# A decoder layer on one Trainium2 core: places of their own for three output-weight tiles, and query tiles that begin on half of the blocks

## What is computed

```python
proj = x @ w_in                                   # 1024 x 8208
y_a = rms_norm(gla(q_a, k_a, v_a, decay)) * silu(r_a)
y_b = attention(rope(q_b), rope(k_b), v_b)        # 8 heads, causal
y = sigmoid(gate_a) * y_a + sigmoid(gate_b) * y_b
x1 = layer_norm(ALPHA * x + y @ w_out, ln1_g, ln1_b)
qry = x1 @ w_q                                    # 8 heads x 2 x 128
s = einsum('nhpd,pkd->nhpk', qry, sub_keys)       # 2 x 128 scores for each head
# top 16 of each half, top 16 of their sums: expert ids and softmax gates
hid = gelu(x1 . u_tab[expert]);  h = sum(gate * hid * v_tab[expert])
out = layer_norm(ALPHA * x1 + h, ln2_g, ln2_b)
```

## Time and profile before

| | us |
|---|---|
| median of 3 runs (1089.97 to 1090.32) | 1090.04 |
| the profiled execution | 1089.23 |
| its span, first to last instruction | 1087.4 |
| PE busy | 1071.9 (99%) |
| DVE busy | 791.6 (73%) |
| ACT busy | 610.2 (56%) |
| POOL busy | 173.0 (16%) |

### The profile page before, as it was taken

The page is one execution under the profiler, slowest core; times in us unless marked ns, Lnnn a source line. Parts: engine busy times, 40 slices in busy tenths (PEclk is TensorE's granted clock), DMA queues, the critical chain, the costliest instruction groups (busy, mean ns, idle before and its releaser), DMA issues.

```text
span 1087.4 us, 18011 instructions
## 1 busy us (share of the span) xinstructions
PE 1071.9 (99%) x5604; PEld 905.8 (83%) x5604; DVE 791.6 (73%) x1516; ACT 610.2 (56%) x1114; POOL 173.0 (16%) x120
## 2 busy tenths in 40 slices
PE   9999999999999999999999999999999999999996
PEld 6887888687888888888888999988888888888885
DVE  4457767387999989899999988875555555555556
ACT  4337645465556756666676666665455555545553
POOL 3040002203000002233224445510000000000001
PEclk9999999999999999999999999999999999999999
DMA  8554444253455554444444434445666555555553
GB/s 281 186 193 161 134 152 145 97 174 136 155 172 187 187 189 159 171 155 160 168 155 139 151 135 142 148 155 194 203 203 207 198 193 193 193 193 193 193 193 116
DMA packets 52857, 186.48 MB, mean 171 GB/s; under 512 B 6336, under 2 KB 6976, under 8 KB 52816
## 3 DMA queue, kind: packets, MB, share of 16 engines
q1 hardware_dynamic: 51152, 181.82, 49.3%
q0 software_dynamic: 944, 3.15, 0.8%
q10 hardware_dynamic: 720, 1.05, 0.3%
HBM read 184.94 MB, written 1.05 MB: 171 GB/s over the span
## 4 chain that ended last, share of the span: by engine, by line
PE 72%; issue 12%; POOL 6%; DVE 5%; DMA 2%; ACT 2%; POOLq 0%; ACTq 0%; SPq 0%; DVEq 0%
PE ps L1514 13%; PE ps L1611 10%; PE ps L1610 10%; PE ps L1612 10%; PE ps L1516 7%; POOL hot_j L464 5%; PE ps L1266 5%; PE ps L1268 4%; PE ps L1267 4%; PE ps L1565 3%; DVE wlo L788 1%; PE ps L1327 1%; ACT whi L487 1%; DMA xraw<-xT 1%; DMA raw<-w_tiles_in 1%
## 5 line engine op out<-in xcount | busy, mean ns | idle before, releaser
L788 DVE TENSOR_TENSOR wlo<-raw,whi 128x1024 fp32r<-128x1024 f32 x341 | 427.0, 1253 | 247.6 <-ACT whi L487 245.2
L487 ACT ACTIVATE whi<-raw 128x1024 fp32r<-128x1024 f32 x343 | 363.2, 1060 | 292.3 <-DMA raw<-w_tiles_v 165.3
L1514 PE MATMUL ps<-pair,whi 128*128 128x512 f32 x1152 | 412.8, 401 | 0.1
L1516 PE MATMUL ps<-pair,wlo 128*128 128x256 f32 x1152 | 321.5, 279 | 0.0
L1514 PEld LDWEIGHTS ps<-pair,whi 128*128 128x128 f32 x1152 | 216.4, 188 | 47.7 <-issue 0.3
L1516 PEld LDWEIGHTS ps<-pair,wlo 128*128 128x128 f32 x1152 | 217.3, 189 | 0.0
L1610 PE MATMUL ps<-whi,hhi 128*128 128x512 f32 x512 | 199.3, 389 | 0.4 <-DVE wlo L788 0.4
L1612 PE MATMUL ps<-whi,hlo 128*128 128x512 f32 x512 | 199.2, 389 | 0.0
L1611 PE MATMUL ps<-wlo,hhi 128*128 128x512 f32 x512 | 199.2, 389 | 0.0
L464 POOL TENSOR_TENSOR hot_j<-raw_ij,gateT 128x512 f32<-128x512 bf16 x64 | 120.0, 1875 | 334.1 <-DVE raw_ij L1171 334.1
L671 ACT ACTIVATE low<-ps 128x256 f32<-128x256 f32 x144 | 55.1, 383 | 137.4 <-PE ps L1516 136.0
(11 more groups left out here) (212 smaller groups left out, 891.2 us busy)
## 6 DMA issues: line engine op xcount, KB each, us to landing
raw<-w_tiles_u SPq DMA_DIRECT2D x128, 512.0 KB, 3.2
raw<-w_tiles_v SPq DMA_DIRECT2D x128, 512.0 KB, 3.2
raw<-w_tiles_in SPq DMA_DIRECT2D x63, 512.0 KB, 3.3
raw<-w_tiles_q SPq DMA_DIRECT2D x16, 512.0 KB, 3.2
raw<-w_tiles_out SPq DMA_DIRECT2D x8, 512.0 KB, 3.2
xt<-x POOLq DMA_DIRECT2D x1, 1024.0 KB, 7.2
raw<-w_tiles_in SPq DMA_DIRECT2D x2, 256.0 KB, 4.4
xraw<-xT SPq DMA_DIRECT2D x2, 256.0 KB, 7.6
```

The costliest lines, as they stand in the source:

```text
L487: act.activation(whi[:, tile.slot, :], raw[:, tile.slot, :], ACT.Copy)\
L788: dve.tensor_tensor(wlo[:, tile.slot, :], raw[:, tile.slot, :], whi[:, tile.slot, :].bitcast(F32), ALU.subtract)\
L1514: pe.matmul(ps[:, bank, :], whi[:, tile.slot, cols], pair[:, k, :, :].rearrange("p a n -> p (a n)"), start=k == 0, stop=False)
L1516: last = pe.matmul(ps[:, bank, SEQ:2 * SEQ], wlo[:, tile.slot, cols], ahi[:, k, :], start=False, stop=k == KC - 1)
```

## The change

**Places of their own.** Out tiles 5, 6 and 7 no longer go through the ring. They get buffers in memory that the attention has finished with (`apart_raw`, `apart_hi`, `apart_lo`), semaphores of their own, and loads which SP issues between the last eight tiles of `w_in`. So T_Q falls from 72 to 69: q tile 0 waits for the slot of out tile 1, q tiles 1 and 2 for those of 2 and 3, q tile 3 for that of out tile 4, and q tile 4 for that of q tile 0.

**Tail.** The out tail is four tiles instead of three.

**Order of ACT, POOL and DVE.** ACT's copies of q tiles 0, 1 and 2 all stand ahead of the norm. POOL makes the low parts of all three ahead of its share of the norm. DVE no longer treats both column halves of token half 1 at each step but one after the other, with x1's low parts 0 and 1 between; the last norm takes the new order too.

**q tiles 0 to 2 on half of the blocks.** Once parts 0 and 1 are there, PE runs blocks 0 to 3 of q tile 0, in three groups of 256-column matmuls, then of q tiles 1 and 2, with the transposes of parts 2 and 3 between; then blocks 4 to 7 of the three.

```diff
+APART, Q_AHEAD = 3, 3
-T_Q = T_OUT + TILES_OUT
+T_Q = T_OUT + TILES_OUT - APART
-TAIL = 3
+TAIL, TAIL_OUT = 3, 4
...
+        loads(0, TILES_IN - 2 * NS, w_tiles_in, 1)
+        for m in range(TILES_IN - 2 * NS, TILES_IN):
+            load(Tile(m), w_tiles_in[m, :, :])
+            n, odd = divmod(m - (TILES_IN - 2 * NS), 2)
+            if odd and n < APART:
+                sp.wait_ge(S["gl_mm"], 1)
+                sp.dma_start(apart_raw[n][:, :], w_tiles_out[TILES_OUT - APART + n, :, :])\
+                    .then_inc(apart_full[n], 16)
...
-        split_lo_q(Tile(T_Q))
+        for n in range(Q_AHEAD):
+            split_lo_q(Tile(T_Q + n))
         pool.wait_ge(S["in_ln1"], 32)
         ln_apply(0, g1b, b1b, "ln_done0")
-        split_lo_q(Tile(T_Q + 1))
...
-        for k in range(TILES_OUT - AHEAD + 1):
-            split_hi(Tile(T_OUT + k + AHEAD))
+        for k in range(TILES_OUT - AHEAD + Q_AHEAD):
+            n = k + AHEAD - (TILES_OUT - APART)
+            if n < 0:
+                split_hi(Tile(T_OUT + k + AHEAD))
+            elif n < APART:
+                apart_high(n)
+            else:
+                split_hi(Tile(T_Q + n - APART))
...
-        norm(0, OUTB, LN1_BANKS, "x1_bank", "g1_ready", T_Q, "ln_done")
-        x1_low()
+        norm(0, OUTB, "x1_bank", ("out_done", 1))
+        dve.wait_ge(S["g1_ready"], 4)
+        weigh(0, LN1_BANKS)
+        root(0)
+        shifted(0, LN1_BANKS, "ln_done")
+        weigh(1, LN1_BANKS)
+        x1_low(0)
+        x1_low(1)
+        shifted(1, LN1_BANKS, "ln_done")
+        x1_low(2)
+        x1_low(3)
+        dve.sem_inc(S["lo_ready"], Q_AHEAD)
...
-        by_pairs(Tile(T_Q), HID[0], True)
+        turn_x1(0)
+        turn_x1(1)
+        blocks, slot = range(KC // 2), Tile(T_Q).slot
+        pe.wait_ge(S["act_split_hi"], X_PARTS + 4 + 2)
+        for k in blocks:
+            cols = slice(k * P, (k + 1) * P)
+            pe.matmul(ps[:, HID[0], 0:SEQ], whi[:, slot, cols], ahi[:, k, :], start=k == 0, stop=False)
+            pe.matmul(ps[:, HID[0], SEQ:2 * SEQ], wlo[:, slot, cols], ahi[:, k, :], start=False, stop=False)
+        turn_x1(2)
+        pe.wait_ge(S["act_split_lo"], X_PARTS + 4 + 2)
+        for k in blocks:
+            cols = slice(k * P, (k + 1) * P)
+            pe.matmul(ps[:, HID[0], SEQ:2 * SEQ], whi[:, slot, cols], alo[:, k, :], start=False, stop=False)
         pe.wait_ge(S["lo_first_q"], 2)
-        for k in range(4):
+        pairs(Tile(T_Q + 1), HID[1], blocks)
+        turn_x1(3)
+        pe.wait_ge(S["lo_first_q"], 3)
+        pairs(Tile(T_Q + 2), HID[2], blocks)
+        pe.wait_ge(S["act_split_lo"], X_PARTS + 4 + 4)
+        for k in range(Q_AHEAD):
+            pairs(Tile(T_Q + k), HID[k], range(KC // 2, KC)).then_inc(S["tiles_used"], 1)
+            if k > 0:
+                scores(k - 1)
+        for k in range(Q_AHEAD - 1, 4):
             by_pairs(Tile(T_Q + k + 1), HID[(k + 1) % 4])
             scores(k)
```

More of the change, by code:

```diff
@@ L330, in layer @@
     raw_full = [S[f"raw_full{n}"] for n in range(NS)]
+    apart_full = [S[f"apart_full{n}"] for n in range(APART)]
     in_xT = [S[f"in_xT{n}"] for n in range(X_PARTS)]
@@ L1001, in _, with norm @@
                 y_low(3)
-        def norm(n, banks, gain, bank_done, gain_ready, tiles, done):
+        def norm(n, banks, bank_done, last_done):
             def total(t, half):
@@ L1028, in norm, with weigh @@
             total(1, 0)
-            dve.wait_ge(S["tiles_used"], tiles)
+            dve.wait_ge(S[last_done[0]], last_done[1])
             total(1, 1)
             variance(1)
-            dve.wait_ge(S[gain_ready], 4)
-            halves = [slice(half * CW, (half + 1) * CW) for half in range(2)]
-            for half, cols in enumerate(halves):
-                own.step(dve.scalar_tensor_tensor(out=xt[:, 1, cols], in0=xt[:, 1, cols], scalar=mv[:, 1, 0:1],
-                                                  in1=ps[:, gain[0] + half, :], op0=ALU.subtract, op1=ALU.mult))
+        def weigh(half, banks):
+            xs = xt[:, 1, half * CW:(half + 1) * CW]
+            own.step(dve.scalar_tensor_tensor(out=xs, in0=xs, scalar=mv[:, 1, 0:1], in1=ps[:, banks[0] + half, :],
+                                              op0=ALU.subtract, op1=ALU.mult))
@@ L1037, in norm, with root @@
+        def root(n):
             dve.wait_ge(S["ln_sqrt"], NT * n + 2)
             own.do(dve.reciprocal(rstd[:, 1:2], rstd[:, 1:2]))
[L1039 to L1053 removed]
@@ L1055, in _, with shifted, x1_low @@
-        dve.wait_ge(S["in_x"], 16)
-        norm(0, OUTB, LN1_BANKS, "x1_bank", "g1_ready", T_Q, "ln_done")
-        x1_low()
+        def shifted(half, banks, done):
+            own.wait()
+            xs = xt[:, 1, half * CW:(half + 1) * CW]
+            dve.scalar_tensor_tensor(out=xs, in0=xs, scalar=rstd[:, 1:2], in1=ps[:, banks[1] + half, :],
+                                     op0=ALU.mult, op1=ALU.add).then_inc(S[done], 1)
+        def x1_low(n):
+            j, t = divmod(n, NT)
+            dve.wait_ge(S["act_split_hi"], X_PARTS + 4 + n + 1)
+            part = (slice(None), slice(4 * j, 4 * j + 4), slice(t * P, (t + 1) * P))
+            dve.tensor_tensor(alo[part], ps[:, OUTB[2 * t + j], :].rearrange("p (k n) -> p k n", n=P),
+                              ahi[part].bitcast(F32), ALU.subtract).then_inc(S["act_split_lo"], 1)
@@ L1254, in _ @@
             split_lo(Tile(m))
-        norm(1, VB, LN2_BANKS, "out_bank", "g2_ready", T_END, "out_ready")
+        norm(1, VB, "out_bank", ("tiles_used", T_END))
+        dve.wait_ge(S["g2_ready"], 4)
+        weigh(0, LN2_BANKS)
+        root(1)
+        shifted(0, LN2_BANKS, "out_ready")
+        weigh(1, LN2_BANKS)
+        shifted(1, LN2_BANKS, "out_ready")
     @block.tensor
@@ L1487, in _ @@
         for half in range(2):
-            for k in range(TILES_OUT - TAIL, TILES_OUT):
-                last = out_half(Tile(T_OUT + k), k, 1, (half,))
-                if half == 1:
+            for k in range(TILES_OUT - TAIL_OUT, TILES_OUT):
+                last = out_half(k, 1, (half,))
+                if half == 1 and k < TILES_OUT - APART:
                     last.then_inc(S["tiles_used"], 1)
+                if half == 1 and k == TILES_OUT - 1:
+                    last.then_inc(S["out_done"], 1)
             if half == 0:
```

101 lines of the change are left out of this document (56 added, 45 removed).

## The result

The changed kernel takes 1092.76 us (median of 8 runs, 1091.99 to 1095.17) against 1089.99 (8 runs beside them, 1088.53 to 1090.73): a ratio of 1.003, interval 1.0021 to 1.004. It is **slower, by 2.8 us**. The predicted time was 1091.8, 1.75 above the kernel before; the measured one lies in the predicted range, but beyond the border of 0.2%, where I had given "slower" only 0.28. In a second batch the same kernel took 1092.44, 1.0021 (1.0012 to 1.003), 2.2 us more than before.

A forecast was written before the change was run, and what follows sets the result against it. PE was taken to bound the kernel. Q tile 1's scores, held by q tile 4's later load, come 1.75 us late, the out stage's 0.1 included: median 1090.04 becomes 1091.8 us, range 1090.1 to 1093.0.

The forecast's parts named there:

- the border of 0.2%: Whole kernel: about 2.2 us, the least a measurement can tell from no change; slower begins at 1092.2 us.
- What bounds it, and the mark: PE, busy 1071.9 of 1087.4 us, bounds; delay of q tile 1's scores, at 268.37 us before, is the kernel's loss.
- Out stage, +0.1: Out tiles: wait at tile 7 goes, 0.68 us wait at tile 5 comes; stage ends 252.75 instead of 252.63.
- (d): Rival: apart loads or their waits hold a w_in or out tile; one landing of 3.3 us, 1095; chance 0.02.
- (c): Rival: POOL's first low part starts before DVE's third; PE waits 2.5 us at out tile 7; 1094.3; chance 0.03.
- 256-column matmuls: First halves of q tile 0: 0.115 us each; if each waited for a weight load, twelve cost 0.9 us more.
- the chain of 5.33 us from q tile 0 to the scores of q tile 1: q tile 4's load, ACT's copies, DVE's query: q tile 0 ends 2.25 us later, PE idles 2.2, mark +1.75.
- Rival (a): Scores of q tile 1 not held, load and copies being quicker; mark at 267.9, time 1089.5; chance 0.14.
- It stays hidden: Norm: POOL, stretched by DVE's subtraction, may be 0.5 us later in everything, yet its x1 parts come before PE wants them.
- It costs from the point at which the granted clock of the pause reads below 1.00: Rival: clock falls to 1.2 GHz in PE's pause before q tile 1's scores; +2.8 us more, 1094.6; chance 0.05.
- The sum: Whole kernel: +1.75 us, out stage's +0.1 included; median from 1090.04 to 1091.8.
- same: Whole kernel: time within what a measurement cannot tell from no change, up to 1092.2 us; chance 0.70.

The follow-up runs named there:

- low_first: Changed kernel with ACT copying the low products of q tiles 1 and 2 ahead of its copies of q tiles 4 and 5; 1091.15 us, 1.0009 of the kernel before.
- whole: Changed kernel, but PE makes all four transposes first and then does q tiles 0 to 2 whole; 1090.89 us, 1.0006 of the kernel before.
- one_input: Changed kernel with DVE's shift rewritten to one tensor operand and a per-partition scalar; 1091.80 us, 1.0021 of the kernel before.
- after: The changed kernel itself, first batch, against the kernel before; 1092.76 us, ratio 1.003.
- after_again: The changed kernel unaltered, run again in a second batch against the kernel before; 1092.44 us, ratio 1.0021.
- two_then: Changed kernel with POOL making the low part of q tile 2 behind its share of the norm; 1091.56 us, 1.0014 of the kernel before.
- warm_q: Changed kernel with nine unused matmuls filling PE's pause ahead of the scores of q tile 1; 1091.99 us, 1.0017 of the kernel before.

## Why the prediction was right and wrong

- **What bounds it, and the mark: right.** The delay of the scores of q tile 3 against the kernel before orders the kernels nearly as their times do (0.1 us: +0.2 and +0.3; 0.3 to 0.9: +0.7 to +0.9; 1.7 to 2.4: +1.7 to +2.3; 3.8 and 3.9: +2.2 and +2.8). No trace shows that time was given back later.
- **Out stage, +0.1: right.** PE waits 0.67 us (forecast 0.68) at the first apart tile instead of at out tile 7, and the stage takes 0.15 us more. No PE wait on the apart loads is to be seen; (d) and (c) did not happen.
- **256-column matmuls, and the chain of 5.33 us from q tile 0 to the scores of q tile 1: right.** They go 0.12 us apart, the chain takes 5.30 us, the pause is 2.05 us (forecast 2.2), and low_first removes it. Rival (a) is out.
- **"It stays hidden", said of POOL's work ahead of the norm: the step that failed first.** I followed POOL's queue and its ports against DVE's large subtraction and did not look at what small instructions of DVE fall into POOL's 7.6 us. `shift` did, with two tensor operands in SBUF: 1.76 us for 0.16. Through DVE's own order, in which the sums of token half 1 stand behind it, it delayed the first transposes of that half by 0.6 us and the mark by 0.4 to 0.6; only in whole, which has all four transposes first, did it also show through ACT and POOL. With it repaired (one_input) the mark is 17.38 for a computed 17.35.
- **"It costs from the point at which the granted clock of the pause reads below 1.00": the condition was right, its chance was not.** I took the end of the kernel as evidence that the clock outlives a pause of 2 us, and gave the fall 0.05. It fell in about one execution in four or somewhat more, and in both profiled ones; it fell after pauses of 2.05 and 1.95 us (after, after_again) and did not after 2.02 and 2.18 (one_input, two_then). My price of 2.8 us for it was too high, measured 1.56. The Trainium skill (TensorE: Matmul & The Clock Gate, section "Part 1: The HAM clock gate") says of the warm-up at a kernel's start that the number of slow matmuls varies from run to run of one kernel. Behind this pause, too, executions of one kernel differ. One place in the kernel where the clock survived a gap was no evidence for another.
- **The sum.** Forecast 1.75, +0.5 for the shift (from the marks), +0.4 for the clock on the mean: an estimate of 2.7, where 2.8 and 2.2 were measured. The two terms that I had at nothing are enough to carry it over the border of 0.2%; that each of them moves the median by so much, the times do not show, because one_input (+2.3) and warm_q (+1.8) are too near the changed kernel's.
- **The balance.** My chance of "same" at 0.70 rested on a sum 0.45 us below the border, with every small omission adding in one direction. With PE busy nearly all the time, a missed wait could only add.

## What to carry to other kernels

Work that starts earlier in halves also ends later: with a ring of slots, ask when the last half frees the slot, and what stands behind that load in each engine's order. Before long instructions are packed onto POOL, list every DVE instruction in that time with two tensor operands in SBUF, the 128x1 ones too, and write those with a scalar operand or keep them out. A pause of 2 us of PE is to be costed with a chance that the clock falls behind it, and a sum that ends just below a border, all of whose omissions are waits, belongs above it.

## What the runs showed of the hardware that I had not expected

- A DVE instruction of one element per partition, with two tensor operands in SBUF, took 1.76 to 1.78 us in five traces while POOL's 128x1024 subtraction ran; with one tensor operand and a scalar it took 0.21 in two traces, under the same subtraction.
- After a pause of about 2 us the granted clock read 0.50 and then 0.66 or 0.68 in the next two stretches of 2 us in some executions, and stayed at 1.00 in others.
- Three loads of 0.52 MB issued at 264.79, 266.2 and 268.0 us (low_first) could be used at 267.93, 270.04 and 272.66, so 2.1 and 2.6 us one after the other; the stretches of 2 us from 266 to 274 moved 231 to 270 GB/s.
- Behind the q tiles a pair of matmuls took 0.353 us in four traces and 0.347 in eight, at a granted clock of 1.00 in all: 1.4 us, also between two executions of the same code.
- What stays open: what decides in which executions the clock falls, and in which the pair takes 0.353 us.
